# A two-block layer on one Trainium2 core: weights and norm of the next stage moved into the stage ahead, and attention scores of two heads issued side by side

## The reference

```python
def hybrid_layer(x, ...):                      # first block
    h = rms_norm(x, norm_pre_w)
    proj = h @ w_in
    moba_out = moba_attention(q, k, v) * silu(a_z)     # 8 heads of 64
    gdn_out = rms_norm(gated_delta_rule(...), gdn_norm_w) * silu(d_z)
    mixed = concatenate([moba_out, gdn_out]) @ w_out
    return x + rms_norm(mixed, norm_post_w)

# second block
h = x
h = h + token_mixers(rmsnorm(h, norm1_g), w_in, ..., w_out)
h = h + peer(rmsnorm(h, norm2_g), w_q, sub_keys, u_tab, v_tab)
return rmsnorm(h, final_g)
```

## Time and profile before

| what | us |
|---|---|
| median of 3 runs | 2410.72 |
| lowest and highest | 2405.76 and 2411.18 |
| the profiled execution: its time | 2405.64 |
| its span in the profile | 2403.9 |
| mean granted clock of TensorE | 0.952 of full speed |

### The profile page before, as it was taken

One profiled execution on the slowest core, in us unless ns is written; L12 is line 12 of the kernel. 1 busy time (PEld: TensorE's weight loads), 2 busy tenths in 40 slices (PEclk: granted clock), 3 DMA queues, 4 the chain that ended last, 5 costly groups with the idle time before them and its releaser, 6 DMA issues. The chain is left out here.

```text
span 2403.9 us, 36262 instructions
## 1 busy us (share of the span) xinstructions
PE 2158.7 (90%) x11207; PEld 1887.0 (78%) x11207; DVE 1690.5 (70%) x3352; ACT 819.6 (34%) x1408; POOL 771.1 (32%) x677
## 2 busy tenths in 40 slices
PE   5998988475999997796979999999998999999997
PEld 4776677364777776686879999999997888888885
DVE  3675545536877763499478888788876888888886
ACT  4443322212222230423424444444432333333333
POOL 1000033000000000147546877887753222222220
PEclk9998999787999998898989999999998999999999
DMA  4431100013424222602256878878688999999995
GB/s 112 83 70 36 18 1 0 22 58 87 112 63 126 63 55 70 199 20 78 95 178 228 295 249 273 295 254 267 227 299 304 333 335 339 337 337 339 336 339 205
DMA packets 229948, 428.88 MB, mean 178 GB/s; under 512 B 18516, under 2 KB 155892, under 8 KB 229620
## 3 DMA queue, kind: packets, MB, share of 16 engines
q1 hardware_dynamic: 170976, 254.85, 34.1%
q0 software_dynamic: 41472, 151.01, 18.3%
q10 hardware_dynamic: 17428, 22.14, 2.6%
HBM read 381.80 MB, written 46.14 MB: 178 GB/s over the span
## 5 line engine op out<-in xcount | busy, mean ns | idle before, releaser
L1847 PE MATMUL bank<-xt_hi,u_hi 128*128 128x384 f32 x896 | 309.3, 345 | 0.0
L2127 PE MATMUL bank<-xt_hi 128*128 128x512 f32 x768 | 302.3, 394 | 7.6 <-DVE xt_lo L2056 7.6
L1847 PE MATMUL bank<-xt_hi,u_lo 128*128 128x384 f32 x896 | 300.6, 336 | 0.0
L1847 PE MATMUL bank<-xt_lo,u_hi 128*128 128x384 f32 x896 | 300.1, 335 | 0.0
L2127 PE MATMUL bank<-xt_hi,xt_lo 128*128 128x512 f32 x768 | 299.8, 390 | 0.0
L2127 PE MATMUL bank<-xt_lo,xt_hi 128*128 128x512 f32 x768 | 299.8, 390 | 0.0
L1709 POOL DMA_INDIRECT row_slot<-in_peer_v_dram,row_index x128 | 139.2, 1088 | 392.7 <-DVE row_x L2060 373.4
L2103 ACT ACTIVATE xt_hi<-xh 128x1024 fp32r<-128x1024 f32 x128 | 135.8, 1061 | 338.4 <-PE bank L2127 332.9
L1378 POOL TENSOR_TENSOR k_wlo<-k_raw,k_whi 128x2048 fp32r<-128x2048 f32 x4 | 18.4, 4604 | 615.8 <-ACT k_whi L1498 615.8
L2053 DVE TENSOR_TENSOR xt_lo<-xh,xt_hi 128x1024 fp32r<-128x1024 f32 x128 | 156.9, 1226 | 83.8 <-ACT xt_hi L2103 82.4
L1788 POOL TENSOR_TENSOR u_two<-u_match,u_weight_hi 128x512 fp32r<-128x512 f32 x96 | 179.7, 1872 | 96.8 <-DVE u_match L1874 96.3
(11 more groups left out here) (430 smaller groups left out, 4908.1 us busy)
## 6 DMA issues: line engine op xcount, KB each, us to landing
xh<-in_peer_v_dram SPq DMA_DIRECT2D x128, 512.0 KB, 5.4
xh<-in_peer_u_dram SPq DMA_DIRECT2D x113, 512.0 KB
x_raw<-in_w_in_dram SPq DMA_DIRECT2D x56, 512.0 KB, 7.0
v_ga<-acts SPq DMA_DIRECT2D x128, 192.0 KB, 5.4
acts<-xh ACTq DMA_DIRECT2D x112, 192.0 KB
weights<-u_spread POOLq DMA_DIRECT2D x32, 512.0 KB
v_gg<-weights SPq DMA_DIRECT2D x128, 128.0 KB
p_raw<-in_w_in_dram SPq DMA_DIRECT2D x12, 1024.0 KB
```

The lines of the kernel that those rows point to most:

```text
L1847: mm = pe.matmul(k.ps[4 + b][:, 0:DENSE], w[b][:, c, :], x[:, c, 0:DENSE], start=(c == 0 and w is uhi and x is hi), stop=(c == DC - 1 and ...
L2127: mm = pe.matmul(k.ps[q][:, :], h[b][:, t * P:(t + 1) * P], v[b][:, f], start=False, stop=False, skip_group_check=True)
```

## The change

Five parts:

- In `attention` the steps are ordered so that the two heads of a pair (b = 0 and 1) follow each other for each query tile, and TensorE issues the scores of both in every second step.
- `gate_and_turn` loads the first two chunks of the output weights of "o1", and DVE makes `m_m` of chunk c + 1 before it waits for the copy of chunk c.
- `project_out` takes its first two chunks from buffers that are already full. It squares the finished tiles of `k.xh` on ACT, one after the other, while DVE makes the next, and takes the root for the norm that follows, into `norm_stat`. "o1" also loads the 7 first sections of `mixers`.
- The stage "n2" is gone; `mixers` runs the norm at its start, with the split of the first section between `scale` and `lows` on DVE, and loads the two first chunks for "o2" at its end.
- `choose_experts` starts with `scale`, and makes the high and low part of the first query weights, then those of the norm, then those of the second query weights.

```diff
+    def __init__(self, nc, k, tag, out, weight, xs, stat, rooted=False):
+
+        self.k, self.out, self.w0, self.xs, self.stat, self.rooted = k, out, COLS[weight][0], xs, stat, rooted
...
-        dve.wait_ge(self.root, 1)
+        if not self.rooted:
+            dve.wait_ge(self.root, 1)
...
-        steps = [(p, b, qt) for p in range(2) for b in range(2) for qt in range(TT)]
+        steps = [(p, b, qt) for p in range(2) for qt in range(TT) for b in range(2)]
...
-                        if n + 2 < n_steps:
+                        if n % 2 == 0 and n + 2 < n_steps:
                             score(i, n + 2)
+                            score(i, n + 3)
...
+                for c in range(2):
+                    sp.dma_start(raw[c][:, :], io["w_out"][0, c * P:(c + 1) * P, :]).then_inc(s["raw_in"], 16)
+                sp.wait_ge(s["raw_in"], 32)
...
-                for c in range(DC):
+                def gate(c):
+                    if c == DC:
+                        return
                     z = Z0 + c if c < 4 else DZ0 + c - 4
...
+                gate(0)
+                for c in range(DC):
+                    gate(c + 1)
                     dve.wait_ge(s["hi_done"], c + 1)
                     dve.tensor_tensor(lo[:, c, :], m32[:, c % 2, :], hi[:, c, :].bitcast(F32), ALU.subtract).then_inc(s["lo_done"], 1)
...
+def project_out(nc, k, tag, weight, src, raw, stat_next, post=None, next_loads=()):
...
-                for c in range(DC):
-                    if c >= 2:
-                        sp.wait_ge(w_lo[c % 2], c // 2)
+                for c in range(2, DC):
+                    sp.wait_ge(w_lo[c % 2], c // 2)
                     sp.dma_start(raw[c % 2][:, :], weight[c * P:(c + 1) * P, :]).then_inc(raw_in[c % 2], 16)
+                for to, part in next_loads:
+                    sp.dma_start(to, part).then_inc(next_in, 16)
+                if next_loads:
...
-                    dve.wait_ge(raw_in[b], 16 * (c // 2 + 1))
                     if c >= 2:
+                        dve.wait_ge(raw_in[b], 16 * (c // 2))
...
+                for t in range(TT):
+                    act.wait_ge(total, 2 * t + 2)
+                    if t >= 2:
+                        act.wait_ge(total_squared, t - 1)
+                    act.activation(squares[:, t % 2, :], k.xh[:, t, :], ACT.Square, accum_out=stat_next[:, t:t + 1]
+                                   ).then_inc(total_squared, 1)
+                act.wait_ge(total_squared, TT)
+                act.activation(stat_next[:, TT:2 * TT], stat_next[:, 0:TT], ACT.Sqrt, scale=1.0 / D, bias=k.eps[:, 0:1])
...
+def mixers(nc, k, io, src, out, raw, out_raw):
...
+        norm = NormAndTurn(nc, k, "x_norm", src, "norm1",
+                           [work[:, 2 * t:2 * t + 2, :].rearrange("p a n -> p (a n)") for t in range(TT)], k.norm_stat, rooted=True)
...
-                        sp.dma_start(raw[n][:, :, :], w_dram[:, :, bass.ds(i * P + W_COLUMNS[n] * D, P)]).then_inc(raw_in[n], 16)
+                            sp.dma_start(raw[n][:, :, :], w_dram[:, :, bass.ds(i * P + W_COLUMNS[n] * D, P)]).then_inc(raw_in[n], 16)
...
+                for c in range(2):
+                    sp.dma_start(out_raw[c][:, :], io["w_out_2"][0, c * P:(c + 1) * P, :]).then_inc(w_out_in, 16)
+                sp.wait_ge(w_out_in, after(32))
...
-                for n in range(7):
+                norm.scale(dve)
+                split(0, XA, True)
+                norm.lows(dve)
+                for n in range(1, 7):
...
+                norm.tensor(pe)
...
+                norm.highs(act)
...
+        norm = NormAndTurn(nc, k, "k_norm", src, "norm2", xs, k.norm_stat, rooted=True)
...
-                norm.squares(act)
                 high(0)
+                norm.highs(act)
                 high(1)
-                norm.highs(act)
...
-                for sec in range(2):
-                    low(dve, sec)
+                low(dve, 0)
                 norm.lows(dve)
+                low(dve, 1)
...
+            x_raw = [k.sb(f"x_raw{s}", [P, DC, P], ctx=x_right, side="right") for s in range(7)]
+            with ExitStack() as st2, ExitStack() as right:
+                o_raw = [k.sb(f"o1_raw{b}", [P, D], ctx=right, side="right") for b in range(2)]
                 xt = (k.sb("mt_hi", [P, DC, T], F32R, ctx=st2), k.sb("mt_lo", [P, DC, T], F32R, ctx=st2))
-                gate_and_turn(nc, k, io, mixed, proj, xt)
+                gate_and_turn(nc, k, io, mixed, proj, xt, o_raw)
                 k.end_stage()
-                project_out(nc, k, "o1", io["w_out"][0], xt, post=io["norm_post_w"][0])
+                project_out(nc, k, "o1", io["w_out"][0], xt, o_raw, k.norm_stat, post=io["norm_post_w"][0],
+                            next_loads=[(x_raw[n][:, :, :], w_in_2[:, :, W_COLUMNS[n] * D:W_COLUMNS[n] * D + P]) for n in range(7)])
                 k.end_stage()
         with ExitStack() as st:
...
+            o_raw = [k.sb(f"o2_raw{b}", [P, D], ctx=st) for b in range(2)]
...
-                norm_and_turn(nc, k, "n2", xt, "norm1")
+                mixers(nc, k, io, xt, mt, x_raw, o_raw)
                 k.end_stage()
-                mixers(nc, k, io, xt, mt)
-                k.end_stage()
-            project_out(nc, k, "o2", io["w_out_2"][0], mt)
+            project_out(nc, k, "o2", io["w_out_2"][0], mt, o_raw, k.norm_stat)
```

More of the change, by code:

```diff
@@ L121, in refined_rsqrt @@
     chain(dve.tensor_tensor(out, out, tmp, ALU.mult))
-def norm_and_turn(nc, k, tag, out, weight):
-    with ExitStack() as st:
-        xs = k.sb(f"{tag}_xs", [P, TT, D], ctx=st)
-        stat = k.sb(f"{tag}_stat", [P, 4 * TT], ctx=st)
-        norm = NormAndTurn(nc, k, tag, out, weight, [xs[:, t, :] for t in range(TT)], stat)
-        with nc.Block() as block:
-            @block.scalar
-            def _(act):
-                norm.squares(act)
-                norm.highs(act)
-            @block.vector
-            def _(dve):
-                norm.scale(dve)
-                norm.lows(dve)
-            @block.tensor
-            def _(pe):
-                norm.tensor(pe)
 class NormAndTurn:
-    def __init__(self, nc, k, tag, out, weight, xs, stat):
-        self.k, self.out, self.w0, self.xs, self.stat = k, out, COLS[weight][0], xs, stat
+    def __init__(self, nc, k, tag, out, weight, xs, stat, rooted=False):
+        self.k, self.out, self.w0, self.xs, self.stat, self.rooted = k, out, COLS[weight][0], xs, stat, rooted
         self.vec, self.sq, self.root, self.scaled, self.turned, self.his, self.los = (
@@ L961, in _, with gate_and_turn @@
                     act.activation(o[:, c, :], k.ps[3][:, :], ACT.Copy).then_inc(o_kept, 1)
-def gate_and_turn(nc, k, io, mixed, proj, out):
+def gate_and_turn(nc, k, io, mixed, proj, out, raw):
     hi, lo = out
@@ L1024, in _ @@
                     mm.then_inc(s["turned"], 1)
-def project_out(nc, k, tag, weight, src, post=None):
+def project_out(nc, k, tag, weight, src, raw, stat_next, post=None, next_loads=()):
     hi, lo = src
     with ExitStack() as st:
-        raw, whi, wlo = ([k.sb(f"{tag}_{n}{b}", [P, D], dt, ctx=st) for b in range(2)]
-                         for n, dt in (("raw", F32), ("whi", F32R), ("wlo", F32R)))
+        whi, wlo = ([k.sb(f"{tag}_{n}{b}", [P, D], F32R, ctx=st) for b in range(2)] for n in ("whi", "wlo"))
         raw_in, w_hi, w_lo = k.sems(f"{tag}_raw_in", 2), k.sems(f"{tag}_w_hi", 2), k.sems(f"{tag}_w_lo", 2)
-        used, summed = k.sem(f"{tag}_used"), k.sem(f"{tag}_summed")
+        used, summed, next_in, total_squared, total = (
+            k.sem(f"{tag}_{n}") for n in ("used", "summed", "next_in", "total_squared", "total"))
+        squares = k.sb(f"{tag}_squares", [P, 2, D], ctx=st)
         if post is not None:
@@ L1097, in _ @@
                         mm.then_inc(used, 1)
-            if post is not None:
-                @block.scalar
-                def _(act):
+            @block.scalar
+            def _(act):
+                if post is not None:
                     for n in range(2 * TT):
@@ L1115 @@
 ATANH_TERMS = 9
-def mixers(nc, k, io, src, out):
+def mixers(nc, k, io, src, out, raw, out_raw):
     hi, lo = src
@@ L1124, in mixers @@
     with ExitStack() as st:
-        raw, whi, wlo = ([k.sb(f"x_{n}{s}", [P, DC, P], dt, ctx=st) for s in range(7)]
-                         for n, dt in (("raw", F32), ("whi", F32R), ("wlo", F32R)))
+        whi, wlo = ([k.sb(f"x_{n}{s}", [P, DC, P], F32R, ctx=st) for s in range(7)] for n in ("whi", "wlo"))
         w_gate = k.sb("x_w_gate", [P, 2, P], ctx=st)
-        tile = lambda n: k.sb(f"x_{n}", [P, T], ctx=st)
-        xc, r, ig, tau, den, e, a, mult, h, ge, vb, cv, yb, sa, sb_ = (
-            tile(n) for n in ("xc", "r", "ig", "tau", "den", "e", "a", "mult", "h", "ge", "vb", "cv", "yb", "sa", "sb"))
+        work = k.sb("x_work", [P, 15, T], ctx=st)
+        xc, r, ig, tau, den, e, a, mult, h, ge, vb, cv, yb, sa, sb_ = (work[:, n, :] for n in range(15))
```

(2 more changed lines are left out.)

27 lines of the change are left out of this document (14 added, 13 removed).

## The result

The changed kernel takes 2367.4 us (median of 4 runs, 2366.4 to 2373.7) against 2408.2 before (4 runs beside it, 2404.8 to 2411.2): a ratio of 0.984, with a 95% interval of 0.981 to 0.986. The profiled execution took 2366.4 us with a span of 2364.6, so 39.3 us less span than before; 2373 us and 33.4 us had been forecast.

The account below looks back on a forecast made before the run. The kernel was taken as stages ending at barriers, each seam bound by its last wait, attention by TensorE. 5.9 + 4.3 + 5.6 + 10.9 + 4.2 + 2.5 = 33.4 us off 2405.6 gives 2372.2, put at 2373; range 2360 to 2385.

Parts of the forecast that it names:

- first rival: In attention: the two heads' scores overlap, one of four passes of a pair hidden, 4.2 us, giving 2369 us; chance 0.20.
- Attention, 5.9 forecast: In attention: pairing scores saves 4.5 us of tiling-form changes and 1.4 us of TensorE waits; bounds nothing and 10.1.
- Fewer changes of form: In attention: TensorE goes to the 64-partition form and back 14 fewer times at 0.32 us each, 4.5 us.
- The stalls: In attention: TensorE's 0.44 us wait for the exponential in a quarter's first step, four times, shrinks by 0.35 each, 1.4 us.
- second rival: Attention gives nothing, because quarters of two narrow and two wide tiles wait for VectorE and ScalarE: 2379 us; chance 0.13.
- gate_and_turn, 4.3: End of gate_and_turn: the next m_m fills seven VectorE gaps of 0.69 us, less 0.08 each: 4.3 us, bounds 3.6 and 4.8.
- First project_out, 5.6: Start of the first project_out: with full buffers VectorE's first cast starts at once instead of waiting for weights, 5.6 us.
- Norm and start of mixers, 10.9: From first project_out's last addition into mixers: first product 9.9 us earlier, plus 1.0 of clock; bounds 9.9 and 11.4.
- third rival: The early loads don't hide, sharing the queue with chunks due; 4.0 us at mixers come back, 2377 us; chance 0.06.
- Second project_out, 4.2: Start of the second project_out: VectorE's 5.17 us wait for weights goes except the stage's end, 4.2 us, bounds 4.0 and 4.4.
- choose_experts, 2.5: Start of choose_experts: squares leave the path, the first query load becomes the last wait; keys turned 2.5 us earlier, bounds 1.0 and 3.0.
- fourth rival: In attention: the granted clock falls from 0.90 to half speed for the whole stretch, 89 us more, 2467 us; chance 0.02.

## Why the prediction was right, and where it was off

Direction, range and nearly every seam were right; the predicted 2373 lies 6 us above the measured 2367.4, and one term makes that. In that term the forecast's own mechanism came true, and beside it, larger than the forecast's, that of the first rival, which had been given a chance of 0.20.

**Attention, 5.9 forecast, 13.5 measured.** The step that failed is the one that left the overlap out of the sum; even the term's upper bound, 10.1, was too low. "Fewer changes of form" was a real part and rightly sized (with two scores of one head side by side 7.0 us of busy time go, by my split 4.5 of them for the changes and 2 for the clock, and the rows give 4.3 for the changes). But the first rival, two heads beside each other, holds, and its size was half of the truth: I took one of four passes for hidden, 4.2 us, and two of four are, 8.6 us. The pair takes exactly what one head takes, 0.70 and 0.70 us with 256 keys, so no count of passes was needed. The stalls went the other way: 1.4 us were to be gained, and 2.4 were lost (idle 12.7 to 15.2). The new order brings most of it, 1.9 us where it is alone, with the same 0.78 us. The forecast had looked for a narrower exponential or the cover of two scores of 512 keys; but in a quarter of wide tiles the exponential got wider, `weigh` ahead of it shorter, and the two scores, since they overlap, cover no more than one. (The trace of before has the wait of 0.44 five times, not four.) That wait is the wait which the second rival feared, in its place but far too small to take the gain. The clock gave what the sum didn't have: 0.90 to 0.92 by the windows, 25 to 18 us at half speed, 3.6 us. In sum 4.5 + 8.6 - 2.4 + 3.6 = 14.3 against 13.5; 0.8 us stay unassigned, and the split between changes and clock is argued from windows rounded to 0.01 of a clock, not shown apart.

The Trainium skill (TensorEngine Tiling (Array Packing), Key Properties) says that different tiles can execute weight loads and matmuls in parallel. The traces agree: two scores of 384 keys in two halves take 0.85 us to the next instruction, as long as 128 and 256 keys in one half, which is 384 keys one after the other. The prediction named the rule, but had no row of before for it and gave it less than it says.

**gate_and_turn, 4.3 and 4.5.** Right, and shown by its undoing.

**First project_out, 5.6 and 5.6.** Right; the cast waits 0.78 us for the barrier alone.

**Norm and start of mixers, 10.9 and 11.1.** Right as a sum: 9.4 up to the first product, where the eight low parts took 6.0 instead of 5.8 us, and 1.7 of clock behind it, forecast 1.0: the granted clock of the 96 matmuls went from 0.92 to 1.00. The first product is busy 0.49 us and not 0.80 as in the earlier trace rows. The third rival, that the early loads don't hide, falls, and more than that: they are not needed.

**Second project_out, 4.2 and 3.9.** Right, if 0.1 under its lower bound: the end of mixers costs VectorE 1.29 us of waiting now, where up to 1.2 had been allowed. The 1.0 us from the first cast to the first addition, at a granted clock of 0.94 instead of 0.92, wasn't forecast and isn't shown to be the change's; between two executions of the changed kernel this stretch moves by more (42.4 us in one, 43.9 in the other, at 0.91).

**choose_experts, 2.5 and 1.2.** Inside its bounds. The step that failed is halving the landing of the second MB: the first doesn't land after half of 9.0 us but after 6.1. The turning of the keys itself also takes longer, 3.67 us instead of 3.22 before, behind a longer wait of TensorE (5.3 and 4.3 us), and the ledger loses 0.3 us up to the first scores.

**The fourth rival**, a clock that falls in attention, didn't show: 0.92.

## What to carry to other kernels

Where two products use only 64 of the 128 rows, look whether they lie in different halves of the partitions and can be issued next to each other: the second was free here, but only with both conditions, and the order that brings them together may open waits on other engines. A load in the stage ahead is worth what still waits for it when the rest of the change is in, so look at the last wait again afterwards: here the loads for mixers were worth nothing, and those for the queries, which the change left out, 5 us. Compare stretches rather than spans when the question is of 3 us, because the same code reached attention anywhere from 187.0 to 191.3 us in these traces; and take them short and from several traces, because a stretch of 43 us moved by 1.5 us by itself.

## What the runs showed of the hardware that was not expected

- Two float32 products of depth 64 in different halves of the partitions, issued one behind the other into two banks, take the time of one: 0.70 us for 2 x 256 keys, 0.92 for 2 x 384, 1.13 for 2 x 512. In the same half 128 and 256 keys take 0.92.
- Of two loads of 1 MB issued together the first landed after 6.1 us and the second after 9.1 (both in the version with the old order in choose_experts): the second MB costs 3 us more, not as much again.
- The same 16 turns took 3.67 us at a granted clock of 0.50 when TensorE had been idle for 5.3 us, and 1.97 at 1.00 when it had been idle for 1.8: shortening a wait by 3.5 us gave 1.7 us more by the clock. The 13 traces agree: 2.0 us behind waits of 1.8 and 2.5, 2.7 to 3.5 behind waits of 4.1 to 4.5, and 3.7 behind all waits from 5.1 to 8.2.
